# Routing weights of a PEER layer: written to DRAM one column at a time by indirect DMAs, in place of one-hot matmuls

## The chip, the cores and the metric

One core of one Trainium2 chip runs the whole layer in one launch. The metric is the device time in microseconds (us) of that launch; lower is better. All data is float32. Wide matrix products are made of three passes of the reduced type fp32r (high part times high part, high times low, low times high), so every operand is split into a high part, rounded by ScalarE, and a low part, the difference.

## The reference

One layer (DEPTH = 1) over 512 latent tokens of 2048 channels and 256 context tokens: token mixing (latent attention and a Fourier branch), then channel mixing by PEER, a retrieval over 128 x 128 = 16384 single-neuron experts. The change is in the second part:

```python
def _peer(h, wq, keys, u, v):                       # T = 512 tokens, 8 heads, 16 experts per head
    q = (hf @ wq).reshape(T, PEER_HEADS, 2, PEER_HALF)
    s = jnp.einsum('thpd,hpkd->thpk', q, keys)      # 2 x 128 scores per head
    s1, i1 = lax.top_k(s[:, :, 0], 16); s2, i2 = lax.top_k(s[:, :, 1], 16)
    cand_s = s1[..., :, None] + s2[..., None, :]    # 256 pairs of a head
    cand_i = i1[..., :, None] * 128 + i2[..., None, :]
    top_s, pos = lax.top_k(cand_s, 16)
    idx = take_along_axis(cand_i, pos); w = softmax(top_s)
    a = einsum('td,thkd->thk', h, u[idx])           # u, v: 16384 x 2048
    coef = w * gelu(a)
    return einsum('thk,thkd->td', coef, v[idx])
```

Each token so chooses 128 experts (slots). Two heads of one token can choose the same expert; its weights then add up.

## The kernel before, in words

The tokens are handled in two ways. The first 128 tokens (TS) **gather**: for each of the 128 slots GpSimd issues an indirect DMA that fetches 128 rows of u (1 MB, one row per token), VectorE forms the dot product with h (`dots`, L1673), and later the same is done with rows of v, which VectorE adds into an accumulator (`axpy`, L1686). The other 384 tokens (TD) are computed **densely** against all experts:

- Up stage: 128 blocks i of 128 experts. SyncE loads the block of u (`pu`, 1 MB, two buffers). TensorE transposes it in four quarters into PSUM (`pre_turn`, L2175), two quarters per half h. ScalarE copies a half to SBUF (`pre_copy`, L1049), then rounds it to the high part (`pre_hi`, L1056), GpSimd subtracts to get the low part (`u_low`, L698), and TensorE multiplies (`pre_up`, L114 to L116). ScalarE applies GELU (`pre_gelu`, L1061) and SyncE stores the result to `gelu_scratch`. TensorE transposes block i+1 quarter by quarter between the products of block i.
- Top-k, on VectorE during the first 26 blocks (`top_experts`, one call per 128 tokens, a chain of 21 linked steps with an exponential from ScalarE in it).
- Routing, during the next 24 blocks: `chosen` is transposed, VectorE builds one-hot matrices for four tokens at a time (96 groups; `one_hots`, L1651 to L1657), TensorE multiplies them (L2235, L2236) into a 128 x 128 map of weights per token, ScalarE copies the map out (`keep_route`, L1096), and SyncE stores it to `route_scratch` in 24 stores with runs of 256 B. The product sums duplicates by itself. Gathers of u begin after these stores have landed, because the gather ring lies over the tiles of the map.
- Down stage: 64 pairs of blocks times two halves of the channels, so 128 steps n. Each step loads 1 MB of v and 384 KB each of `gelu_scratch` and `route_scratch`; VectorE multiplies the last two (`down_coef`, L1692), ScalarE rounds v and the coefficients, VectorE takes their low parts (`down_v_lo`, `down_coef_lo`, both L1407), TensorE runs 36 matmuls of 512 columns. The `axpy` steps of the gathered tokens are put between, one per step at first and six per five steps in the second half.

The order on every engine is written out by hand: each engine runs its list in order and waits on semaphore counts. So a wait on VectorE for a gathered row also holds everything that VectorE has after it. GpSimd's list is `u_low` for both halves of a block, with one gather after five of six halves once routing is over (`gather_u`, L707), then the gathers of v (L712), which wait for a free ring buffer (four of them). SyncE's list is the loads and stores; v and coefficients for the first two down steps are fetched some 70 blocks before the end of the up stage.

## Time and profile before

| | us |
|---|---|
| median of 3 runs (lowest, highest) | 4923.87 (4911.05, 4928.48) |
| profiled execution, own time | 4906.7 |
| its span, first to last instruction | 4905.0 |
| mean granted TensorE clock, share of full | 0.963 |
| PE busy, share of the span | 4509.8 (92%) |
| DVE, ACT, POOL busy | 2843.1, 1638.3, 1395.8 |
| DMA packets, all | 652126 (967.09 MB) |

PE is TensorE (PEld its weight loads), DVE is VectorE, ACT ScalarE, POOL GpSimd, SP SyncE. The median of the runs is 17 us (0.35%) above the profiled execution. A busy PE row is made of overlapping instructions, so 92% doesn't say that TensorE does 92% of what it could: the spacing of its work tells more. In the rows below, a bracket or a last column names what ended the idle time of the engine before an instruction.

### The profile page before, as it was taken

The numbers are of one execution on the slowest core, as the hardware profiler recorded it, in microseconds if no ns is written. First come the engines' busy times: TensorE is split into PE (matmuls) and PEld (weight loads), VectorE is DVE, ScalarE is ACT, GpSimd is POOL, SyncE is SP. The second block draws the span as 40 slices with busy tenths as digits, with TensorE's granted clock in tenths as the row PEclk, the third lists the DMA queues.
The fourth block names the chain that finished last, engine by engine and source line by source line (L and its number), as shares of the span: only waits on it lengthen the run. The fifth ranks groups of instructions, "written<-read, shape, count | busy, mean of one in ns | idle before, by whom it ended". The sixth has DMA issues, their size and how long they took to land.

```text
span 4905.0 us, 61497 instructions
## 1 busy us (share of the span) xinstructions
PE 4509.8 (92%) x23115; PEld 3849.9 (78%) x23115; DVE 2843.1 (58%) x3097; ACT 1638.3 (33%) x1746; POOL 1395.8 (28%) x643
## 2 busy tenths in 40 slices
PE   7899998999989999699999999999996899999997
PEld 2587777777767877588999988999995778777776
DVE  1234665544436643657799954444444677777776
ACT  0322322333331121324446643444442233322222
POOL 0002332000002300223544556777771011011110
PEclk9899999999989999799999999999998999999998
DMA  8325664000015652453326677777776999989994
GB/s 287 96 78 172 182 184 141 18 28 30 32 39 163 189 170 61 140 167 106 122 102 162 160 235 287 290 286 287 292 283 233 349 342 345 335 315 331 338 341 166
DMA packets 652126, 967.09 MB, mean 197 GB/s; under 512 B 122203, under 2 KB 520595, under 8 KB 599571
## 3 DMA queue, kind: packets, MB, share of 16 engines
q1 hardware_dynamic: 610979, 680.35, 42.0%
q0 software_dynamic: 40928, 285.23, 16.1%
q8 instruction: 45, 0.74, 0.1%
q10 hardware_dynamic: 144, 0.52, 0.0%
q14 instruction: 30, 0.25, 0.0%
HBM read 896.82 MB, written 69.21 MB: 197 GB/s over the span
## 4 chain that ended last, share of the span: by engine, by line
PE 55%; DMA 13%; DVE 11%; issue 10%; ACT 6%; POOL 4%; SPq 1%; ACTq 0%; DVEq 0%; POOLq 0%
PE pp L114 16%; PE pp L116 15%; PE pp L115 15%; DMA gel<-gelu_scratch 10%; POOL pTul L698 3%; DVE vDl L1407 3%; PE pp L2175 3%; ACT vDh L1126 2%; DMA wm<-in_w_mod_dram 1%; PE pp L1806 1%; DVE mred L1287 1%; DVE gel L1692 1%; PE pp L1964 1%; DVE acc L1686 1%; PE pp L2236 1%
## 5 line engine op out<-in xcount | busy, mean ns | idle before, releaser
L698 POOL TENSOR_TENSOR pTul<-pT,pTuh 128x1024 fp32r<-128x1024 f32 x256 | 731.5, 2857 | 522.9 <-ACT pTuh L1056 507.2
L114 PE MATMUL pp<-h2h,pTuh 128*128 128x384 f32 x2048 | 732.9, 358 | 18.9 <-POOL pTul L698 17.4
L114 PE MATMUL pp<-vDh,coh 128*128 128x512 f32 x1536 | 614.6, 400 | 108.1 <-DVE col L1407 107.8
L116 PE MATMUL pp<-h2h,pTul 128*128 128x384 f32 x2048 | 691.7, 338 | 0.0
L115 PE MATMUL pp<-h2l,pTuh 128*128 128x384 f32 x2048 | 690.1, 337 | 0.0
L1673 DVE SCALAR_TENSOR_TENSOR ring<-ring,h2tok 128x2048 f32<-128x2048 f32 x128 | 357.6, 2796 | 480.7 <-DMA ring<-in_peer_u_dram,sidx 480.0
L115 PE MATMUL pp<-vDl,coh 128*128 128x512 f32 x1536 | 609.1, 397 | 0.0
L116 PE MATMUL pp<-vDh,col 128*128 128x512 f32 x1536 | 608.5, 396 | 0.0
L674 POOL TENSOR_TENSOR mbuf<-mbuf,silu 128x2048 f32<-128x2048 f32 x64 | 260.5, 4070 | 995.8 <-DMA mbuf<-in_w_mod_dram 995.1
L114 PEld LDWEIGHTS pp<-vDh,coh 128*128 128x128 f32 x1536 | 295.7, 193 | 187.0 <-DVE vDl L1407 73.5
L712 POOL DMA_INDIRECT ring<-in_peer_v_dram,sidx x128 | 151.7, 1186 | 938.2 <-DVE acc L1686 917.2
L114 PEld LDWEIGHTS pp<-h2h,pTuh 128*128 128x128 f32 x2048 | 388.0, 189 | 27.4 <-POOL pTul L698 27.1
L1202 DVE TENSOR_TENSOR wl<-wraw,wh 128x2048 fp32r<-128x2048 f32 (+1 forms) x97 | 263.0, 2711 | 246.8 <-ACT wh L776 246.7
L1049 ACT ACTIVATE pT<-pp 128x1024 f32<-128x1024 f32 x256 | 265.3, 1036 | 396.3 <-PE pp L2175 394.9
L115 PEld LDWEIGHTS pp<-h2l,pTuh 128*128 128x128 f32 x2048 | 388.8, 190 | 0.0
L116 PEld LDWEIGHTS pp<-h2h,pTul 128*128 128x128 f32 x2048 | 386.7, 189 | 0.0
L1407 DVE TENSOR_TENSOR vDl<-vraw,vDh 128x2048 fp32r<-128x2048 f32 x128 | 293.3, 2291 | 142.5 <-ACT vDh L1126 142.5
L1132 ACT ACTIVATE coh<-gel 128x768 fp32r<-128x768 f32 x128 | 108.5, 847 | 766.1 <-DVE gel L1692 638.4
L116 PEld LDWEIGHTS pp<-vDh,col 128*128 128x128 f32 x1536 | 295.0, 192 | 63.1
L115 PEld LDWEIGHTS pp<-vDl,coh 128*128 128x128 f32 x1536 | 296.0, 193 | 61.1
L2175 PE MATMUL pp<-ident,pu 128*128 128x128 f32 x2048 | 311.5, 275 | 18.7 <-DMA pu<-in_peer_u_dram 17.9
L114 PE MATMUL pp<-hxh,wh 128*128 128x512 f32 x784 | 315.4, 402 | 13.7 <-DVE wl L1202 9.8
(343 smaller groups left out, 8959.7 us busy)
## 6 DMA issues: line engine op xcount, KB each, us to landing
pu<-in_peer_u_dram SPq DMA_DIRECT2D x128, 1024.0 KB, 6.8
vraw<-in_peer_v_dram SPq DMA_DIRECT2D x128, 1024.0 KB, 8.1
mbuf<-in_w_mod_dram SPq DMA_DIRECT2D x64, 1024.0 KB, 5.7
wraw<-in_w_in_dram SPq DMA_DIRECT2D x48, 1024.0 KB, 8.5
wt<-route_scratch SPq DMA_DIRECT2D x128, 384.0 KB, 7.2
gel<-gelu_scratch SPq DMA_DIRECT2D x128, 384.0 KB, 9.1
wm<-in_w_mod_dram SPq DMA_DIRECT2D x16, 2048.0 KB, 8.5
gelu_scratch<-act_g SPq DMA_DIRECT2D x128, 192.0 KB, 1.9
```

The costliest lines, as they stand in the source:

```text
L114: pe.matmul(out, lh, rh, start=first, stop=False)
L115: pe.matmul(out, lh, rl, start=False, stop=False)
L116: return pe.matmul(out, ll, rh, start=False, stop=last)
L674: pool.tensor_tensor(mbuf[s][:, :, :], mbuf[s][:, :, :], silu[:, :, 0:1].to_broadcast([P, DC, P]), ALU.mult).then_inc(mu_prod, 1)
L698: pool.tensor_tensor(pTul[:, c, :], pT[:, c, :], pTuh[:, c, :].bitcast(fp32), ALU.subtract).then_inc(u_lo, 1)
L712: pool.indirect_dma_start(ring[k % 4][:, :], None, v_rows, bass.IndirectOffsetOnAxis(ap=sidx[:, k:k + 1], axis=0)).then_inc(ring_in[k % 4] ...
L1049: act.activation(pT[:, 8 * h:8 * h + 8, :], pp[h][:, :].rearrange("p (c j) -> p c j", c=8), ACT.Copy).then_inc(pre_raw, 1)
L1132: act.activation(coh[s][:, :, :], gel[s][:, :, :], ACT.Copy).then_inc(co_hi, 1)
L1202: dve.tensor_tensor(wl[s][:, 0:n, :], wraw[s][:, 0:n, :], wh[s][:, 0:n, :].bitcast(fp32), ALU.subtract).then_inc(w_lo, 1)
L1407: return dve.tensor_tensor(dst, src, hi.bitcast(fp32), ALU.subtract)
L1673: dve.scalar_tensor_tensor(out=chunks(ring[k % 4]), in0=chunks(ring[k % 4]), scalar=1.0, in1=h2tok[:, :, 0:TS], op0=ALU.mult, op1=ALU.mult ...
L2175: mm = pe.transpose(pb[q][:, P * (c % 4):P * (c % 4) + P], pu[s][:, P * c:P * c + P], ident[:, :])
```

## The change

The one-hot stage goes. After each `top_experts` call for the 384 dense tokens, VectorE runs 128 short instructions: for slot k it compares the token's 128 expert numbers with that of slot k, multiplies by the weights and sums (`accum_out`), which gives the slot the total weight of its expert. GpSimd then writes, with one indirect DMA per slot, 128 single 4 B elements into `route_scratch`, which SyncE has filled with zeros during the attention stage (8 DMAs of 3.1 MB in runs of 2 KB). There are 384 such scatters: 3 after each of blocks 18 to 35 (54), and 3 after each gather from block 36 on, until all are out (330, so 110 gathers). After every 16 scatters GpSimd waits until all earlier ones of its 128 tokens have landed.

Top-k and the summing now take the first 36 blocks (TOPS). From block 36 on ScalarE rounds the high part of u directly from PSUM and VectorE subtracts directly from PSUM (`late_hi`, `u_rest`), so GpSimd's `u_low` and ScalarE's copy end there; a PSUM half is released by VectorE. From block 36 on VectorE does one dot product after each half, in order; after block 102 it does one `axpy` after each half (50 in all), and the other 78 are spread over the down steps, never two in one. The gather ring has three buffers, not four. v and coefficients are prefetched at block 114. In the down steps `axpy` stands before `down_coef`, and ScalarE rounds v before the coefficients.

```diff
+TOPS = 36
+SCATTER_AT = 18
+EXP_AT = (5, 11, 20, 30)
+LINKS = 21
+COEF_AT = 102
+PREFETCH_AT = 114
...
+            def zero_route(p):
+                sp.dma_start(route_flat[:, bass.ds(p * ZROW, ZROW)].rearrange("j (a n) -> j a n", n=512),
+                             zeros[:, :].unsqueeze(1).to_broadcast([P, ZROW // 512, 512])).then_inc(z_stored, 16)
...
+            def gather(k):
+                if k >= 3:
+                    pool.wait_ge(ring_used, k - 2)
+                pool.indirect_dma_start(ring[k % 3][:, :], None, u_rows if k < SLOTS else v_rows,
+                                        bass.IndirectOffsetOnAxis(ap=sidx[:, k % SLOTS:k % SLOTS + 1], axis=0)
+                                        ).then_inc(ring_in[k % 3], 16)
+
+            def scatter(n):
+                b, k = n // SLOTS, n % SLOTS
+                if k == 0:
+                    pool.wait_ge(tk_chosen, b + 3)
+                elif k % TOPK == 0:
+                    pool.wait_ge(r_stored[b], 16 * k)
+                pool.indirect_dma_start(route_cells, bass.IndirectOffsetOnAxis(ap=ridx[b][:, k:k + 1], axis=0),
+                                        rw[b][:, k:k + 1], None).then_inc(r_stored[b], 16)
...
+            for i in range(SCATTER_AT, TOPS):
+                first_lows(i)
+                for _ in range(3):
+                    scatter(n)
+                    n += 1
             pool.wait_ge(tk_chosen, 2)
+            pool.wait_ge(tk_chain, SCORE_READ)
+            for k in range(2 * SLOTS):
+                gather(k)
+                for _ in range(3):
+                    if n < DB * SLOTS:
+                        scatter(n)
+                        n += 1
...
+            def late_hi(i, s, h):
+                act.wait_ge(u_turned, 2 * i + h + 1)
+                if not isinstance(i, int) or i >= TOPS + 2:
+                    act.wait_ge((u_half, a_done)[h], i - 1)
+                elif i == TOPS:
+                    act.wait_ge((u_half, a_done)[h], i)
+                elif h == 0:
+                    act.wait_ge(tk_chosen, 5)
+                act.activation(pTuh[s][:, 8 * h:8 * h + 8, :], pp[h][:, :].rearrange("p (c j) -> p c j", c=8),
+                               ACT.Copy).then_inc(u_hi, 1)
...
+                for k in range(SLOTS):
+                    if k >= 8:
+                        dve.wait_ge(tk_chain, tk.at - 7)
+                    tk.inc(dve.scalar_tensor_tensor(out=same[:, k % 8, :], in0=expert[:, :], scalar=expert[:, k:k + 1],
+                                                    in1=chosen[:, 2, :], op0=ALU.is_equal, op1=ALU.mult,
+                                                    accum_out=rw[b - 1][:, k:k + 1]))
...
+            def u_rest(i, h):
+                s = i % 2
+                c = slice(8 * h, 8 * h + 8)
+                dve.wait_ge(u_hi, 2 * i + h + 1)
+                lo(pTul[s][:, c, :], pp[h][:, :].rearrange("p (c j) -> p c j", c=8), pTuh[s][:, c, :]).then_inc(u_sub, 1)
...
+            for i in range(TOPS, NK):
+                if i == COEF_AT + 1:
+                    dve.wait_ge(scoef_set, 1)
+                    ch.link(dve.tensor_tensor(scoef[:, :], scoef[:, :], sw[:, :], ALU.mult))
+                for h in range(2):
+                    u_rest(i, h)
+                    if k < SLOTS:
+                        dot(k)
+                        k += 1
+                    elif i > COEF_AT:
+                        axpy(k - SLOTS)
+                        k += 1
...
             def ax_before(n):
+                return min(SLOTS, in_up + max(n - 2, 0) * (SLOTS - in_up + 1) // (NK - 10))
...
             for n in range(2, NK):
-                down_coef(n)
                 for k in range(ax_before(n), ax_before(n + 1)):
                     axpy(k)
+                down_coef(n)
                 down_v_lo(n)
```

## Rows read from the trace of the kernel before

**Rows 1.** The page: the chain that ended last, share of the span by engine

```profile
PE 55%; DMA 13%; DVE 11%; issue 10%; ACT 6%; POOL 4%; SPq 1%; ACTq 0%; DVEq 0%; POOLq 0%
```

**Rows 2.** Stretches (us): length, busy of PE, PEld, DVE, ACT, POOL, clock, DMA share, GB/s

```profile
2243.00:2516.00 273.00, 270.23 (x1701) 265.44 (x1700) 218.77 (x815) 131.83 (x147) 134.65 (x52) 1.00 0.32 116
2516.00:2879.00 363.00, 351.59 (x2434) 347.90 (x2435) 329.97 (x386) 211.18 (x227) 178.25 (x51) 0.99 0.62 154
2879.00:3688.00 809.00, 782.61 (x4849) 764.24 (x4847) 353.99 (x252) 345.29 (x379) 614.81 (x281) 0.99 0.77 286
3790.00:4300.00 510.00, 486.94 (x2120) 398.56 (x2119) 371.19 (x238) 155.84 (x118) 53.47 (x57) 0.98 0.94 341
4300.00:4870.00 570.00, 523.36 (x2213) 425.54 (x2212) 422.31 (x273) 164.45 (x124) 88.87 (x63) 0.96 0.85 311
```

**Rows 3.** Timeline of ACT, GELU of blocks 0, 25, 51, 127; start, duration

```profile
2254.22 0.49 ACT L1061 ACTIVATE act_g<-pp 128x384 f32<-128x384 f32 x1
...
2515.51 0.49 ACT L1061 ACTIVATE act_g<-pp 128x384 f32<-128x384 f32 x1 [1.06 <-PE pp L116]
...
2879.09 0.49 ACT L1061 ACTIVATE act_g<-pp 128x384 f32<-128x384 f32 x1 [1.07 <-PE pp L116]
...
3687.81 0.49 ACT L1061 ACTIVATE act_g<-pp 128x384 f32<-128x384 f32 x1 [5.20 <-PE pp L116]
```

**Rows 4.** The same, two GELUs five blocks apart in the late up stage

```profile
3007.52 0.49 ACT L1061 ACTIVATE act_g<-pp 128x384 f32<-128x384 f32 x1 [1.06 <-PE pp L116]
...
3058.32 0.49 ACT L1061 ACTIVATE act_g<-pp 128x384 f32<-128x384 f32 x1 [1.15 <-PE pp L116]
```

**Rows 5.** Timeline of POOL at the up stage's end: indirect DMAs in a row

```profile
3684.68 2.92 POOL L707 DMA_INDIRECT ring<-in_peer_u_dram,sidx  x1 [0.30 <-issue]
3687.90 0.93 POOL L712 DMA_INDIRECT ring<-in_peer_v_dram,sidx  x1 [0.30 <-issue]
3689.14 2.65 POOL L712 DMA_INDIRECT ring<-in_peer_v_dram,sidx  x1 [0.30 <-issue]
```

**Rows 6.** Timeline of DVE in the same stretch: the dot products

```profile
3684.50 2.29 DVE L1673 SCALAR_TENSOR_TENSOR ring<-ring,h2tok 128x2048 f32<-128x2048 f32 x1 [3.54 <-DMA ring<-in_peer_u_dram,sidx]
...
3688.69 2.29 DVE L1673 SCALAR_TENSOR_TENSOR ring<-ring,h2tok 128x2048 f32<-128x2048 f32 x1 [1.90 <-DMA ring<-in_peer_u_dram,sidx]
```

**Rows 7.** Groups of 2861:3680: count, busy us, mean ns, idle before and its releaser

```profile
L1673 DVE SCALAR_TENSOR_TENSOR ring<-ring,h2tok 128x2048 f32<-128x2048 f32 x125 | 350.7, 2809 | 473.9 <-DMA ring<-in_peer_u_dram,sidx 473.2
...
L707 POOL DMA_INDIRECT ring<-in_peer_u_dram,sidx x126 | 195.0, 1548 | 19.1 <-issue 10.0
```

**Rows 8.** DMA issues of the whole run: KB each, median us to landing

```profile
gelu_scratch<-act_g SPq DMA_DIRECT2D x128, 192.0 KB, 1.9
...
ring<-in_peer_u_dram,sidx POOLq DMA_INDIRECT x128, 7.3
```

**Rows 9.** Timeline of POOL in the top-k stretch: a low part of u

```profile
2270.39 2.39 POOL L698 TENSOR_TENSOR pTul<-pT,pTuh 128x1024 fp32r<-128x1024 f32 x1 [2.35 <-ACT pTuh L1056]
```

**Rows 10.** Timeline of DVE at the end of the first top-k call

```profile
2305.93 0.29 DVE L1633 SCALAR_TENSOR_TENSOR sidx<-tk_chosen 128x128 uint32<-128x128 f32 x1
```

**Rows 11.** Timeline of DVE, low part of v in two pairs of down steps

```profile
3889.71 2.29 DVE L1407 TENSOR_TENSOR vDl<-vraw,vDh 128x2048 fp32r<-128x2048 f32 x1 [0.53 <-ACT vDh L1126]
...
4287.62 2.29 DVE L1407 TENSOR_TENSOR vDl<-vraw,vDh 128x2048 fp32r<-128x2048 f32 x1 [2.79 <-ACT vDh L1126]
...
4341.04 2.28 DVE L1407 TENSOR_TENSOR vDl<-vraw,vDh 128x2048 fp32r<-128x2048 f32 x1
...
4793.69 2.29 DVE L1407 TENSOR_TENSOR vDl<-vraw,vDh 128x2048 fp32r<-128x2048 f32 x1 [2.28 <-ACT vDh L1126]
```

**Rows 12.** Timeline of PE: the down stage's first matmul, and two of a later step

```profile
3698.69 0.77 PE L114 MATMUL pp<-vDh,coh 128*128 128x512 f32 x1 [10.92 <-DVE col L1407]
...
4054.28 0.39 PE L114 MATMUL pp<-vDh,coh 128*128 128x512 f32 x1
4054.51 0.39 PE L115 MATMUL pp<-vDl,coh 128*128 128x512 f32 x1
```

More of the change, by code:

```diff
@@ L634, in _ @@
                     coef_loads(2 * i + s, s, 1)
-            for b in range(TB):
-                sp.wait_ge(fin_set, b + 1)
-                sp.dma_start(out[0, P * b:P * b + P, :], acc[:, b, :]).then_inc(fin_stored, 16)
+            sp.wait_ge(fin_set, 1)
+            sp.dma_start(out[0, 0:TS, :], accs[:, :]).then_inc(fin_stored, 16)
+            for b in range(DB):
+                sp.wait_ge(fin_set, b + 2)
+                sp.dma_start(out[0, TS + P * b:TS + P * b + P, :], acc[:, b, :]).then_inc(fin_stored, 16)
             sp.wait_ge(fin_stored, 16 * TB)
@@ L717, in _ @@
                 u_low(i, 1)
-            pool.wait_ge(tk_chosen, 2)
-            for ss in r_stored:
-                pool.wait_ge(ss, 64 * (TD // RT // 2) + 16)
-            k = 0
-            for i in range(LATE + 2, NK):
-                for h in range(2):
-                    u_low(i, h)
-                    if k < SLOTS and (2 * i + h) % 6 != 5:
-                        gather_u(k)
-                        k += 1
-            while k < SLOTS:
-                gather_u(k)
-                k += 1
@@ L1078, in top_block, with late_block @@
                 pre_hi(i + 1, 1)
-            for i in range(TK_FIRST):
-                top_block(i, i % 2, 1 if i == 5 else None)
+            def late_block(i, s):
+                late_hi(i + 1, 1 - s, 0)
+                pre_gelu(i, s)
+                late_hi(i + 1, 1 - s, 1)
+            for i in range(TOPS - 1):
+                top_block(i, i % 2, EXP_AT.index(i) + 1 if i in EXP_AT else None)
                 if 2 <= i < 6:
@@ L1667, in chunks, with dot @@
             def chunks(t):
                 return t[:, :].rearrange("p (c d) -> p c d", c=DC)
-            dve.wait_ge(h2_hi, DC + 4)
-            for k in range(SLOTS):
-                dve.wait_ge(ring_in[k % 4], 16 * (k // 4) + 16)
-                dve.scalar_tensor_tensor(out=chunks(ring[k % 4]), in0=chunks(ring[k % 4]), scalar=1.0,
+            def dot(k):
+                dve.wait_ge(ring_in[k % 3], 16 * (k // 3) + 16)
+                dve.scalar_tensor_tensor(out=chunks(ring[k % 3]), in0=chunks(ring[k % 3]), scalar=1.0,
@@ L2165, in _, with pre_turn @@
             mod_sum(63, 1, 6, 30)
-            def pre_turn(i, s, q):
+            def pre_turn(i, s, q, late=False):
                 if q == 0:
@@ L2214, in _ @@
             pe.wait_ge(mu_set, 4)
-            for i in range(TK_FIRST):
+            for i in range(TOPS):
                 pre_block(i, i % 2)
```

325 lines of the change are left out of this document (115 added, 210 removed).

## The prediction

> **What bounds the kernel now.** I read the chain of waits by engine first, then the stretches, then the spacing of TensorE's work. The chain lies 55% on TensorE [rows 1], and TensorE is busy for nearly all of the three up-stage stretches at a clock of 0.99 or 1.00 [rows 2]. Only the spacing says how much of that is needed. Five clean blocks of the late up stage take 3058.32 - 3007.52 = 50.8 us, so 10.16 us a block, 5.08 a half [rows 4]. The three stretches between the GELUs of blocks 0, 25, 51 and 127 take 261.3, 363.6 and 808.7 us for 25, 26 and 76 blocks: 10.45, 13.98 and 10.64 us a block [rows 3]. Over 127 x 10.16 = 1290 us the up stage loses 143 us: 7 in the top-k part, 99 in and behind routing, 37 later. In the down stage a matmul starts every 0.23 us, so a step of 36 needs about 8.2 us [rows 12]. The steps take 397.9 / 47 = 8.47 us in the first half and 452.7 / 49 = 9.24 in the second [rows 11], and the first one starts 10.9 us after the up stage ends [rows 12]. GpSimd is 76% busy in the late up stage (614.8 of 809) [rows 2]; there VectorE spends 473 us waiting for gathered rows, with the products themselves at 351 us [rows 7]. So gathering, not arithmetic, is what VectorE waits for already.
>
> **The parts that remove work.** Without one-hot matmuls, map copies, map stores and the late start of the gathers, the 99 us behind routing can go. With at most one axpy in a step, 78 rather than 128 of them, and axpy placed where VectorE waits for coefficients, I let the down steps come to 8.25 us: 47 x 0.22 + 49 x 0.99 = 59 us, rounded down to 57 because a few waits for transfers will stay. The start of the down stage no longer waits for the last dot products, since these end near block 88 to 97: 10.9 us become about 2, a gain of 9. The down stage gives 66 us; bounds are 20 (the second half stays at 9.2 because it is limited by transfers, DMA share 0.85) and 75 (every step at 8.17).
>
> **The zeros** are 25 MB in 8 stores during attention, where the page shows the DMA engines mostly idle; I take nothing. If a weight load were held by the 3.1 MB ahead of it at the 341 GB/s of [rows 2], that is 9 us each, 74 us in all at the very worst; the load goes ahead of the zeros in the queue and has a whole attention pair to land, so this stays out.
>
> **Blocks 0 to 35.** At the top-k pace, 35 intervals x 10.45 = 366 us. Added are 54 scatters on GpSimd. An indirect DMA in a row with others takes 0.93 us and 0.30 of issue, 1.24 in all [rows 5]; three are 3.7 us. They stand in front of the next low part, ahead of which GpSimd idles 2.35 us [rows 9], so up to 1.4 us a block is late and TensorE waits: about 1 us x 18 = 18, and 3 waits for landing of some 2 us, 24 us together (bounds 0 and 50). Sum: 390 us. VectorE runs beside it: four top-k calls, in the old stretch 219 us busy [rows 2], some 57 each with the part before it, and 384 summing instructions. The nearest row is a 128 x 128 operation of two inputs, 0.29 us [rows 10]; with the accumulator read, 0.37, so 142 us. 228 + 142 = 370, plus the 14 us or so that a call waits for the exponential: 384, just inside 390. The bounds are 0.21 and 0.6 us an instruction (GpSimd and VectorE delaying each other), so no stall or up to 75 us of it before block 36, where ScalarE waits for the last sum.
>
> **Blocks 36 to 88, the step that decides.** GpSimd must issue one gather and three scatters for each dot product, and VectorE's list takes one dot product per half block, in order with the subtraction that feeds TensorE. So TensorE's half can't be shorter than T, the time of GpSimd for four indirect DMAs. The trace shows no scatter; it has the same number of descriptors as a gather (one per partition), so I take the gather's 1.24 us; the bounds are 0.93 (no issue gap) and 1.9 us (the landing of a small store [rows 8], were GpSimd to wait for it). Four make 4.96 us: alone they would just fit in 5.08.
> They are not alone. The indirect DMA issued at 3684.68 began under a dot product (3684.50 to 3686.8) and took 2.92 us: it got through only 0.8 us after that had ended. The one at 3689.14 did the same (2.65), while the one at 3687.90, already under way when the product began, took 0.93 [rows 5, 6]. Over the stage the mean is 1.55 us [rows 7]. With GpSimd always issuing, each product catches one issue: in the mean the product's 2.29 less half an issue interval, 0.62; I take 1.6 us. T = 4.96 + 1.6 = 6.56.
> Then there are the waits for landing, one per 16 scatters, 20.6 in this stretch. A scatter is queued behind a gather that takes 7.3 us to land, and a lone small store takes 1.9 [rows 8]; I take 3.5, less 0.8 because a dot product can pass meanwhile: 2.7 x 20.6 / 110 = 0.5. T = 7.06 us, for 110 gathers, 53 blocks: 106 x 7.06 = 748 us.
> The Trainium skill (SBUF — State Buffer, Who interferes with whom) says that a `tensor_tensor` probe did not stall a GpSimd-issued DMA, since descriptor generation needs the write interface, as it infers. By that, T would be 5.08. The same section says that a VectorE instruction with two SBUF inputs contends with a GpSimd instruction that reads SBUF, and the indirect DMA reads its indices there: the 2.92 us row stands with this second rule.
>
> **Blocks 89 to 127** carry only gathers: 39 x 10.64 = 415 us, the old late pace, prefetch hiccup included. VectorE then does 2.4 us of product and some 1.1 us of subtraction per half, ScalarE less than before, and neither is near 5.08. That the low part (2.4 us) leaves GpSimd I count at nothing, since 10.64 contains only 0.5 us of waits of any kind. The ring of three is enough: 7.3 us to landing and 2.4 of product are 9.7, against 15.2 for three halves; without that room a half would be 9.7 / 3 = 3.2 us at least, so it never binds. Two added waits are covered likewise: VectorE's for the gathered tokens' GELU at block 103, which ScalarE computes once the products are over, has blocks 98 to 102 as cover (51 us; behind it stand the subtractions, so TensorE would stop), and SyncE's for all scatters at block 114 comes 25 blocks after the last of them.
>
> **Sum.** 390 + 748 + 415 = 1553 us against 1433.6: +119. Down stage -66. Net +53 on the profiled 4906.7: 4960. The runs' median is 17 us above that execution, so the forecast is 4977 us. In general, net = 106 T - 695 us; it is zero at T = 6.55.
>
> **Rivals.**
> *GpSimd keeps up* (T of 5.08 to 5.7). For it: four issues are 4.96 us, and two thirds of the gathers now go unblocked (a mean of 1.55 is 0.95 with 1.9 more for one in three [rows 5, 7]). Against it: the blocked rows, and that 0.12 us of room holds no landing wait. All falls to -156, with no delay before block 36 -180: 4744 to 4850 by the median.
> *GpSimd binds mildly* (T 5.7 to 6.4), if a scatter is nearer to 1.0 us or the landing waits cost nothing: 4850 to 4925.
> *The small packets or VectorE's sums are dear* (slower still). Each half brings 24 packets of 4 B per DMA engine. Routing's stores, 24 of 1 MB in 98304 packets of 256 B, took share 0.62 at 154 GB/s, where the later stage's ratio would give the block loads 0.23: 23 ns a packet [rows 2], so 0.6 us a half. If one costs 240 ns (1.9 us for eight), 5.8 us come on top of 4.5 of other traffic (1.67 MB at 286 GB/s per 0.77 of share): T = 10.3 and +397. From 50 ns the landing waits grow, T passes 7.6 near 130 ns. Or the sums cost 0.6 us each and stall 75 us. 5045 to 5250 and beyond.
> The Trainium skill (DMA: Bandwidth & Descriptors, Specifications) says that below 512 B the engine does a read-modify-write. It gives no price for 4 B; by its rule the dear end is nearer, and no trace here shows it.
> *The change doesn't do what it says*: GpSimd would still have to wait on something of routing; none is left in its list.
>
> **Chances.** Forecast (T 6.4 to 7.5; 4925 to 5045) 0.49; mild 0.14; keeps up 0.21; dear 0.16. The range leaves out half of the best case and half of the dearest: 4790 to 5110; the likeliest case's own is 4925 to 5045. About 0.3%, 15 us, can be told from no change. Faster takes keeps up and nearly all of mild, with a little for a larger down-stage gain: 0.35. Same: 0.1. Slower: 0.55.
>
> **What would show it.** Right: GELUs of blocks 40 to 85 some 14 us apart, GpSimd nearly always busy or waiting for the landing there, DMA_INDIRECT rows of 2.8 us under dot products, VectorE waiting for `ring`, then about 10.2 us a block from 90 on; down steps at 8.2 to 8.3. Wrong: 10.2 us a block from 36 on (GpSimd keeps up), a gap before block 36 with ScalarE waiting for VectorE (sums), a DMA share near 1 in that stretch (small packets), or a second half of the down stage still at 9.2.

## The result, and the profile after

The changed kernel takes 4946.74 us (median of 13 runs, 4938.44 to 4960.93), the kernel before in the same measurement 4923.87 (13 runs, 4911.05 to 4935.42): a ratio of 1.0052, 95% interval 1.0041 to 1.0063. It is 23 us slower. I had forecast 4977 us, 53 us slower. The sign was right, and so was the mechanism by which the up stage gets longer; the down stage gains more than I had it. The profiled execution of the changed kernel has an own time of 4955.31 us and a span of 4953.5, at a clock of 0.947.

First the chain of the page, to be held against [rows 1]. TensorE's share is larger, and GpSimd has 12% of the chain where it had 4%:

```profile
PE 61%; POOL 12%; DVE 10%; issue 8%; DMA 4%; ACT 3%; SPq 0%; DVEq 0%; ACTq 0%; POOLq 0%
PE pp L116 19%; PE pp L118 18%; PE pp L117 18%; POOL route_scratch L700 8%; DVE tk_same L1623 4%; POOL ring L690 3%; DMA wm<-in_w_mod_dram 1%; PE pp L1793 1%; PE pp L2162 1%; DVE mred L1271 1%; DMA route_scratch<-rw,ridx 1%; PE pp L1951 1%;
```

The GELUs on ScalarE of blocks 0, 35, 36, 88 and 127 give the length of each part, as [rows 3] did before:

```profile
2266.18 0.49 ACT L1065 ACTIVATE act_g<-pp 128x384 f32<-128x384 f32 x1
...
2664.98 0.49 ACT L1065 ACTIVATE act_g<-pp 128x384 f32<-128x384 f32 x1 [9.40 <-remote]
2709.18 0.49 ACT L1065 ACTIVATE act_g<-pp 128x384 f32<-128x384 f32 x1 [8.76 <-PE pp L118]
...
3413.00 0.49 ACT L1065 ACTIVATE act_g<-pp 128x384 f32<-128x384 f32 x1 [6.05 <-PE pp L118]
...
3830.09 0.49 ACT L1065 ACTIVATE act_g<-pp 128x384 f32<-128x384 f32 x1 [1.65 <-PE pp L118]
```

So 398.8 us to block 35, 44.2 for block 36, 703.8 for 52 blocks (13.54 each), 417.1 for the last 39 (10.69 each). The stretches beside them (length; busy of PE, PEld, DVE, ACT, POOL; clock; DMA share; GB/s):

```profile
2250.00:2665.00 415.00, 380.16 (x2339) 371.47 (x2337) 386.69 (x1542) 177.65 (x197) 247.93 (x132) 0.96 0.33 112
2665.00:2709.00 44.00, 13.05 (x65) 12.58 (x66) 26.25 (x74) 2.41 (x3) 25.87 (x21) 0.61 0.41 145
2709.00:3413.00 704.00, 589.75 (x3329) 565.43 (x3327) 354.01 (x310) 126.58 (x157) 540.23 (x417) 0.92 0.71 247
3413.00:3830.00 417.00, 398.23 (x2480) 392.28 (x2480) 250.18 (x170) 96.87 (x119) 65.57 (x70) 0.98 0.81 297
```

In the third one TensorE does the same work as anywhere, in a third more time, and nothing in the columns is full: GpSimd has 540 of 704 us. The clock of 0.92 goes with TensorE's waits; it is 1.00 over these blocks when the waits are gone (e1, below). The groups of that stretch show why that is full all the same (count; busy us, mean ns; idle before, releasers):

```profile
L700 POOL DMA_INDIRECT route_scratch<-rw,ridx x312 | 391.4, 1254 | 132.1 <-issue 91.8 <-DMA route_scratch<-rw,ridx 40.3
...
L1645 DVE SCALAR_TENSOR_TENSOR ring<-ring,h2tok 128x2048 f32<-128x2048 f32 x104 | 238.4, 2293 | 350.2 <-DMA ring<-in_peer_u_dram,sidx 344.8 <-issue 5.4
...
L690 POOL DMA_INDIRECT ring<-in_peer_u_dram,sidx x105 | 149.3, 1422 | 32.0 <-issue 32.0
L2162 PE MATMUL pp<-ident,pu 128*128 128x128 f32 x832 | 139.9, 295 | 114.1 <-DVE pTul L1391 114.0
```

GpSimd's two rows sum to 391.4 + 132.1 + 149.3 + 32.0 = 704.8 us, the whole stretch. "Idle, issue" before an indirect DMA is not free time. The chain runs backwards through the rows: TensorE waits for VectorE's subtraction, which stands behind a dot product, which waits 345 us for gathered rows, which GpSimd issues too slowly. Its timeline in the middle of the stretch:

```profile
3000.87 0.98 POOL L690 DMA_INDIRECT ring<-in_peer_u_dram,sidx  x1 [0.30 <-issue]
3002.15 2.20 POOL L700 DMA_INDIRECT route_scratch<-rw,ridx  x1 [0.30 <-issue]
3004.65 0.96 POOL L700 DMA_INDIRECT route_scratch<-rw,ridx  x1 [0.30 <-issue]
3005.92 0.96 POOL L700 DMA_INDIRECT route_scratch<-rw,ridx  x1 [0.30 <-issue]
3007.18 2.21 POOL L690 DMA_INDIRECT ring<-in_peer_u_dram,sidx  x1 [0.30 <-issue]
3009.70 0.98 POOL L700 DMA_INDIRECT route_scratch<-rw,ridx  x1 [0.30 <-issue]
3015.83 2.71 POOL L700 DMA_INDIRECT route_scratch<-rw,ridx  x1 [5.15 <-DMA route_scratch<-rw,ridx]
```

and VectorE's beside it:

```profile
3001.21 2.29 DVE L1645 SCALAR_TENSOR_TENSOR ring<-ring,h2tok 128x2048 f32<-128x2048 f32 x1 [4.16 <-DMA ring<-in_peer_u_dram,sidx]
...
3006.26 2.29 DVE L1645 SCALAR_TENSOR_TENSOR ring<-ring,h2tok 128x2048 f32<-128x2048 f32 x1 [1.61 <-DMA ring<-in_peer_u_dram,sidx]
```

A scatter costs 0.96 + 0.30 us, as a gather does. The one that begins at 3002.15, under the product of 3001.21 to 3003.50, ends at 3004.35, 0.85 us after the product; so does the gather at 3007.18 (end 3009.39, product's end 3008.55). Of the 416 indirect DMAs of the stretch, the 99 that begin under a product take 2.35 us in the mean, the other 317 take 0.97. The landing wait at 3015.83 is 5.15 us. With 0.96 + 0.30 for each of four, a half block of 6.77 us is 5.04 of issuing, 1.35 of delay under products ((391.4 + 149.3 - 417 x 0.96) / 104) and 0.39 of landing waits (40.3 / 104): 6.78.

The 44 us of block 36 are on VectorE:

```profile
2640.46 0.35 DVE L1623 SCALAR_TENSOR_TENSOR tk_same<-tk_expert,tk_chosen 128x128 f32<-128x128 f32 x1
...
2640.73 2.54 DVE L1623 SCALAR_TENSOR_TENSOR tk_same<-tk_expert,tk_chosen 128x128 f32<-128x128 f32 x1
...
2679.80 0.35 DVE L1623 SCALAR_TENSOR_TENSOR tk_same<-tk_expert,tk_chosen 128x128 f32<-128x128 f32 x1
...
2690.07 2.29 DVE L1645 SCALAR_TENSOR_TENSOR ring<-ring,h2tok 128x2048 f32<-128x2048 f32 x1 [2.95 <-DMA ring<-in_peer_u_dram,sidx]
...
2692.28 1.22 DVE L1391 TENSOR_TENSOR pTul<-pp,pTuh 128x1024 fp32r<-128x1024 f32 x1
```

The last summing instruction is at 2679.80, four products follow, the fourth of them waits for its rows, and only then comes the first subtraction of the new scheme, at 2692.28, for which TensorE has waited 34 us. A lone sum goes by at 0.27 us, but the one at 2640.73 took 2.54. GpSimd had begun a low part just then:

```profile
2640.74 2.39 POOL L680 TENSOR_TENSOR pTul<-pT,pTuh 128x1024 fp32r<-128x1024 f32 x1 [1.46 <-ACT pTuh L1049]
```

The down stage is the gain. Low parts of v on VectorE, steps 6, 63, 66 and 127:

```profile
3910.71 2.29 DVE L1391 TENSOR_TENSOR vDl<-vraw,vDh 128x2048 fp32r<-128x2048 f32 x1 [10.26 <-ACT vDh L1114]
...
4387.82 2.29 DVE L1391 TENSOR_TENSOR vDl<-vraw,vDh 128x2048 fp32r<-128x2048 f32 x1 [1.87 <-ACT vDh L1114]
...
4412.87 2.29 DVE L1391 TENSOR_TENSOR vDl<-vraw,vDh 128x2048 fp32r<-128x2048 f32 x1 [1.09 <-ACT vDh L1114]
...
4910.61 2.29 DVE L1391 TENSOR_TENSOR vDl<-vraw,vDh 128x2048 fp32r<-128x2048 f32 x1 [4.12 <-ACT vDh L1114]
```

That is 477.1 / 57 = 8.37 us a step in the first half and 497.7 / 61 = 8.16 in the second, where the kernel before took, over the same steps of its trace, 8.67 and 9.10. From the last GELU to the end of the span are 1123.4 us, before 1217.2.

### The profile page after: what moved, and what is told of

Its sections match the earlier page's. It is cut to its first block, busy times and chain, and to the rows that moved or that the text cites. A ratio compares the mean times of both kernels' runs of the same rounds, so it can differ in the third digit from the quotient of the medians.

```text
span 4953.5 us, 59127 instructions
## 1 busy us (share of the span) xinstructions
PE 4470.3 (90%) x22338; PEld 3812.0 (77%) x22338; DVE 2831.8 (57%) x3664; ACT 1349.0 (27%) x1465; POOL 1295.3 (26%) x844
## 4 chain that ended last, share of the span: by engine, by line
PE 61%; POOL 12%; DVE 10%; issue 8%; DMA 4%; ACT 3%; SPq 0%; DVEq 0%; ACTq 0%; POOLq 0%
PE pp L116 19%; PE pp L118 18%; PE pp L117 18%; POOL route_scratch L700 8%; DVE tk_same L1623 4%; POOL ring L690 3%; DMA wm<-in_w_mod_dram 1%; PE pp L1793 1%; PE pp L2162 1%; DVE mred L1271 1%; DMA route_scratch<-rw,ridx 1%; PE pp L1951 1%; POOL pTul L680 1%; ACT wh L767 1%; DMA pu<-in_peer_u_dram 1%
## 5 line engine op out<-in xcount | busy, mean ns | idle before, releaser
L116 PE MATMUL pp<-h2h,pTuh 128*128 128x384 f32 x2048 | 753.4, 368 | 18.2 <-POOL pTul L680 18.0
L118 PE MATMUL pp<-h2h,pTul 128*128 128x384 f32 x2048 | 709.6, 346 | 0.0
L117 PE MATMUL pp<-h2l,pTuh 128*128 128x384 f32 x2048 | 708.2, 346 | 0.0
L116 PE MATMUL pp<-vDh,coh 128*128 128x512 f32 x1536 | 603.5, 393 | 40.6 <-DVE col L1391 40.3
L700 POOL DMA_INDIRECT route_scratch<-rw,ridx x384 | 472.8, 1231 | 157.4 <-issue 109.8
L1645 DVE SCALAR_TENSOR_TENSOR ring<-ring,h2tok 128x2048 f32<-128x2048 f32 x128 | 293.1, 2291 | 364.3 <-DMA ring<-in_peer_u_dram,sidx 358.8
L2162 PE MATMUL pp<-ident,pu 128*128 128x128 f32 x2048 | 327.9, 285 | 186.7 <-DVE pTul L1391 154.0
L2162 PEld LDWEIGHTS pp<-ident,pu 128*128 128x128 f32 x2048 | 263.3, 147 | 222.9 <-DVE pTul L1391 172.7
L1114 ACT ACTIVATE vDh<-vraw 128x2048 fp32r<-128x2048 f32 x128 | 245.3, 1917 | 677.4 <-PE pp L118 653.7
L116 PEld LDWEIGHTS pp<-h2h,pTuh 128*128 128x128 f32 x2048 | 403.2, 197 | 21.2 <-POOL pTul L680 13.2
L117 PEld LDWEIGHTS pp<-h2l,pTuh 128*128 128x128 f32 x2048 | 403.5, 197 | 0.0
```

Source lines behind the costliest of these rows:

```text
L116: pe.matmul(out, lh, rh, start=first, stop=False)
L117: pe.matmul(out, lh, rl, start=False, stop=False)
L118: return pe.matmul(out, ll, rh, start=False, stop=last)
L700: pool.indirect_dma_start(route_cells, bass.IndirectOffsetOnAxis(ap=ridx[b][:, k:k + 1], axis=0), rw[b][:, k:k + 1], None).then_inc(r_stor ...
L1114: act.activation(vDh[s][:, :, :], vraw[s][:, :, :], ACT.Copy).then_inc(w_hi, 1)
L1645: dve.scalar_tensor_tensor(out=chunks(ring[k % 3]), in0=chunks(ring[k % 3]), scalar=1.0, in1=h2tok[:, :, 0:TS], op0=ALU.mult, op1=ALU.mult ...
```

## The experiments

The runs in one table. "Half" is half of the mean block between the GELUs of blocks 36 and 88; "up" is from the first GELU to the last; "down" from there to the end of the span. Each kernel ran beside the kernel before; those with the same time in the column "before" ran on one chip together. Where the hand-over is at block 42 (e8, e9, e11, e12), "half" mixes five blocks of the early scheme and the hand-over with the rest; over blocks 42 to 88 alone these four have 6.92, 5.72, 5.56 and 5.60, the kernel after 6.79.

| kernel | before, us | this, us | ratio (95%) | half | up | down |
|---|---|---|---|---|---|---|
| before, profiled | | | | 5.87 | 1433.6 | 1217.2 |
| after, profiled | 4923.87 | 4946.74 | 1.0052 (1.0041-1.0063) | 6.77 | 1563.9 | 1123.4 |
| r1_before_again | 4944.39 | 4940.77 | 0.9997 (0.9985-1.0010) | 5.89 | 1438.9 | 1236.9 |
| e1_no_late_scatters | 4944.39 | 4757.84 | 0.9627 (0.9611-0.9643) | 5.07 | 1365.8 | 1122.7 |
| e2_short_dots | 4944.39 | 4833.49 | 0.9777 (0.9761-0.9793) | 5.80 | 1444.5 | 1125.9 |
| e5_rotated | 4944.39 | 4910.52 | 0.9935 (0.9919-0.9952) | 6.49 | 1515.1 | 1123.6 |
| r2_after_again | 4936.29 | 4947.34 | 1.0018 (1.0007-1.0029) | 6.83 | 1557.0 | 1122.2 |
| e6_before_down_order | 4936.29 | 4864.64 | 0.9848 (0.9830-0.9867) | 5.91 | 1441.7 | 1166.1 |
| e10_old_down_order | 4936.29 | 4980.54 | 1.0080 (1.0059-1.0101) | 6.82 | 1559.3 | 1156.7 |
| e9_all | 4936.29 | 4822.31 | 0.9765 (0.9742-0.9789) | 5.95 | 1437.9 | 1127.9 |
| e3_two_per_gather | 4941.83 | 4870.00 | 0.9856 (0.9840-0.9873) | 6.02 | 1481.6 | 1122.7 |
| e8_tops42_only | 4941.83 | 4939.02 | 0.9996 (0.9983-1.0010) | 7.04 | 1544.2 | 1125.6 |
| e11_no_gap | 4941.83 | 4817.09 | 0.9748 (0.9732-0.9764) | 5.55 | 1423.1 | 1123.9 |
| e12_no_burst | 4940.16 | 4801.96 | 0.9719 (0.9703-0.9735) | 5.59 | 1406.8 | 1125.9 |

**Is the second stretch GpSimd's, and what is in its half block?**

e1 takes the scatters from block 36 on away; it leaves out the 330 late routing weights.

```diff
             for k in range(2 * SLOTS):
                 gather(k)
-                for _ in range(3):
-                    if n < DB * SLOTS:
-                        scatter(n)
-                        n += 1
```

> The changed kernel with the 330 scatters from block 36 on left out (so most routing weights stay zero); the gathers stay. My theory, that four indirect DMAs of GpSimd per half block set the pace (13.5 us a block from 36 to 88): blocks there fall to 10.2 or 10.3 us, 52 x 3.25 = 169 us less, about 4780 us. Rival 1, that the pace comes from VectorE's new place in front of TensorE (a PSUM half is released only after its subtraction, with the dot products in the same list): blocks stay near 13.5 us, about 4945 us. Rival 2, small packets that crowd the DMA engines: the same gain as by my theory; this run doesn't tell the two apart.

e2 leaves the scatters and makes the products short; it leaves out 15 of each dot product's 16 chunks.

```diff
-  dve.scalar_tensor_tensor(out=chunks(ring[k % 3]), in0=chunks(ring[k % 3]), scalar=1.0,
-                           in1=h2tok[:, :, 0:TS], ...
+  dve.scalar_tensor_tensor(out=chunks(ring[k % 3])[:, 0:1, :], in0=chunks(ring[k % 3])[:, 0:1, :],
+                           scalar=1.0, in1=h2tok[:, 0:1, 0:TS], ...
```

> The changed kernel with each dot product taken over the first 128 of 2048 channels only (the rest of it is left out), so VectorE holds its two-operand instruction for some 0.3 us, not 2.29; gathers and scatters are all issued. My theory (the product blocks the start of an indirect DMA, 1.35 us a half, and beside it come 5.06 us of issue and 0.4 of landing waits): a half falls from 6.77 to about 5.5 us, so blocks 36 to 88 from 13.5 to 11.0 us, about 130 us less, 4815 us. Rival (the scatters' small packets delay the gathered rows, or landing waits dominate): the transfers are unchanged, so no change beyond 20 us, about 4935 us.

e5 keeps scatters, products and waits but takes the 16 scatters between two waits from the three blocks of tokens in turn, so that a wait is for scatters of which the last was issued 32 earlier.

```diff
+  order = list(range(3 * (TOPS - SCATTER_AT)))
+  ... # then groups of TOPK from the three token blocks in turn
-  b, k = n // SLOTS, n % SLOTS
+  b, k = order[n] // SLOTS, order[n] % SLOTS
```

> The changed kernel with the order of the scatters from block 36 on changed: groups of 16 of the three token blocks in turn, so that the wait for the landing of earlier scatters of the same tokens is nearly always over when it is reached. Same scatters, same gathers. By the waits of the changed kernel's trace (40 us in 11 waits from block 36 to 88) I expect 30 to 40 us less, 4910 us. Rival (small packets set the pace; the wait only moves to the gathered rows): no change, 4945 us.

Without late scatters the same 52 blocks take 10.14 us each, and TensorE is busy for all of it:

```profile
2705.00:3230.00 525.00, 525.00 (x3315) 518.06 (x3315) 352.00 (x311) 126.43 (x156) 96.34 (x103) 1.00 0.91 329
```

GpSimd's rows of e2 from 2707 to 3310 us, then of e5 from 2704 to 3378 (stretches as long as blocks 36 to 88 are there, but begun 13 us late):

```profile
L700 POOL DMA_INDIRECT route_scratch<-rw,ridx x304 | 294.0, 967 | 162.6 <-issue 88.1 <-DMA route_scratch<-rw,ridx 74.5
L690 POOL DMA_INDIRECT ring<-in_peer_u_dram,sidx x107 | 104.5, 977 | 39.1 <-issue 31.1 <-DVE ring L1645 8.1
```

```profile
L708 POOL DMA_INDIRECT route_scratch<-rw,ridx x306 | 371.3, 1213 | 93.2 <-issue 93.2
L690 POOL DMA_INDIRECT ring<-in_peer_u_dram,sidx x106 | 170.9, 1613 | 37.5 <-issue 31.7 <-DVE ring L1653 5.8
```

In e2 the mean issue is 0.967 and 0.977 us: the delay is gone with the long products, so it was theirs. The landing waits grow from 40.3 to 74.5 us, which gives back 0.33 of the 1.35 us a half; 5.80 is left, where I had written 5.5. In e5 the landing waits are gone and the issues stay long (1.2 and 1.6 us), so a half falls by only 0.28 of the 0.39. The small packets don't set the pace: e2 moves the same packets in 603 us as the kernel after in 704, and its half is made up by GpSimd's own rows. What share they have in the landing waits is not shown. Take all the late scatters away (e1) and TensorE is the bound.

**One scatter less.** e3 has two behind a gather and a third behind every fourth.

```diff
-  for _ in range(3):
+  for _ in range(DB * SLOTS - n if k == SLOTS + 2 else 3 if k % 4 == 0 else 2):
```

> The kernel after with one edit: two scatters behind a gather and a third behind every fourth, rather than three behind each; the last 38 go together behind the third gather of the value rows. Theory (GpSimd's list sets the half block, one scatter costs about 1.26 us of it, landing waits are shared): a half of 6.77 us falls by 0.75 x 1.26 + 0.1 = 1.05 to about 5.7, blocks 36 to 88 at 11.4 us each (-111 us), the scatters and dot products last some ten blocks longer at the same pace (+10), in all 85 to 110 us faster than the kernel after: a ratio of 0.980 to 0.986. Rival (the small packets delay the block loads whatever the issue rate): the pace falls in proportion to the packets only, to 12.7 us a block, and half of that comes back later: under 40 us of gain.

A half falls by 0.75 us, to 6.02, where I expected 5.7: the three quarters of a scatter bring 0.95, but the delay per product grows from 1.35 to 1.49 us (by the same sum from e3's trace), and the landing waits stay (43.8 us). The gain is 82 us of the up stage, a ratio of 0.9856, at the least gain that I had written (0.980 to 0.986). Its rival (under 40 us) is out.

**The hand-over.** e8 moves it to block 42.

```diff
-TOPS = 36
+TOPS = 42
-EXP_AT = (5, 11, 20, 30)
+EXP_AT = (5, 11, 22, 33)
-COEF_AT = 102
+COEF_AT = 106
```

> The kernel after with the hand-over from the top-k scheme to the late scheme at block 42, not 36, and the exponentials of top-k blocks 2 and 3 behind blocks 22 and 33, not 20 and 30. Theory: the sums end near block 37, so ScalarE's wait at the hand-over goes (34 us at block 36), as do its waits of 11 and 15 us at blocks 20 and 30; what is left at the hand-over is the first gather, 20 to 25 us at block 42; 18 scatters more are done before it, so three blocks fewer run at 13.5 us (-9). In all 30 to 55 us faster than the kernel after, a ratio of 0.992 to 0.996. Rival: these waits are covered by VectorE's or GpSimd's later work being the bound anyway (the blocks behind end at the same time): under 10 us of gain.

My expectation failed. Block 36 is reached after 388.2 us, where it was 443.0, but 34 of these us were the hand-over, and it has only moved: block 42 takes 43.0 us, as block 36 took 44.2, where I had expected 20 to 25. VectorE waits there for the rows of four products in a row, 20.5 us for the first. The waits for the exponential shrank and did not go (blocks 23 and 34 take 17.7 and 18.0 us; blocks 20 and 30 took 21.2 and 25.2). GpSimd's first gather comes at 2701.1 us, in the kernel after at 2657.5, and its last scatter at 3419.0, there at 3409.8: the list starts 44 us later and, 18 scatters shorter, takes 34 us less, with three more blocks done at its end. The pace in it is no better (6.92 us a half over blocks 42 to 88, against 6.79). The up stage is only 13 to 20 us shorter than in the two profiles of the kernel after, and the ratio is 0.9996 where the forecast was at most 0.996. Its rival fits best: the later blocks wait for GpSimd's list, and that began later.

e9 is e3, e5 and e8 in one. e11 and e12 follow from its trace.

> The changed kernel mended where the theory says it loses: TOPS 42 rather than 36 (top-k and sums no longer end after the early blocks), the exponentials at blocks 22 and 33 rather than 20 and 30, COEF_AT 106, from there 2 scatters after a gather and 3 after every fourth (the rest after the last gather of u), and the scatter groups of 16 in turn over the three token blocks. Theory: the gap of 34 us at block 36 and 26 us of waits before it go; a half block takes 3.25 issues of 1.27 us and 1.35 of blocking, 5.5 us, so 11 us a block for 62 blocks rather than 13.5 for 52 and 10.2 for 10: about 100 us less; with the landing waits, 150 to 180 us below the changed kernel, ratio to before 0.97. Rival, that dot products and scatters collide as often as there are products, so that fewer scatters per gather don't help: 60 to 80 us less, ratio 0.99.

It came to 4822.31 us, a ratio of 0.9765, where the kernel after has 1.0018 on the same chip: 125 us less, short of the 150 to 180 expected and well over the rival's 60 to 80. Block 42 took 35.3 us, on a wait for the first gathered row:

```profile
DVE ring L1653 <- DMA ring<-in_peer_u_dram,sidx: 40.8, 5, 30.5
ACT pTuh L1067 <- PE pp L2170: 26.7, 1, 26.7
PEld pp L2170 <- DVE pTul L1399: 23.2, 1, 23.2
```

so e11 issues three gathers ahead of block 41's low parts and drops the four products ahead of the first subtraction:

```diff
             for i in range(SCATTER_AT, TOPS):
+                if i == TOPS - 1:
+                    pool.wait_ge(tk_chosen, 2)
+                    pool.wait_ge(tk_chain, SCORE_READ)
+                    for k in range(3):
+                        gather(k)
                 first_lows(i)
 ...
-            while k < 4:
-                dot(k)
-                k += 1
```

> e9_all with two edits: the first three gathers stand ahead of block 41's low parts in GpSimd's list, and the four dot products ahead of the first subtraction of the late scheme are gone (they follow with two a block as the others). Theory: in e9_all block 42 took 35.3 us because VectorE waited 30 us there for the first gathered row and TensorE waited for VectorE; with the gathers on their way before, the block takes 10 to 14 us and the kernel gains 20 to 25 us on e9_all, a ratio of about 0.971 to 0.973. Rival: the top-k's sums are what comes late (VectorE reaches that place too late in any case), then the gap stays at 20 us or more and the ratio at 0.976.

The gap at block 42 went (10.6 us there), but the up stage became only 15 us shorter than in e9 (1423.1 against 1437.9), the ratio 0.9748 against 0.9765, short of the 0.971 to 0.973 expected: block 109 now took 33.0 us.

```profile
POOL ring L690 <- DVE accs L1668: 39.3, 10, 6.8
...
DVE accs L1668 <- DMA ring<-in_peer_v_dram,sidx: 24.0, 2, 23.8
PEld pp L2170 <- DVE pTul L1402: 20.2, 1, 20.2
```

The scatters left over, issued in one go behind the third gather of v (`k == SLOTS + 2` in e3's edit), keep the next gathers of v back: some 28 of them at 1.26 us are 35 us. e12 takes the burst away:

```diff
-  for _ in range(DB * SLOTS - n if k == SLOTS + 2 else 3 if k % 4 == 0 else 2):
+  for _ in range(3 if k % 4 == 0 else 2):
```

> e11_no_gap with one edit: the scatters that are left behind the third gather of the value rows aren't issued in one go there but go on at two behind a gather (a third behind every fourth) until none is left, near block 112. Theory: in e11_no_gap block 109 took 33 us, since VectorE's axpy waited 23.8 us for value rows whose gathers stood behind some 25 scatters in a row (1.26 us each) in GpSimd's list, and TensorE waited for the subtraction behind that axpy. Without the burst the block takes some 11 us and the kernel gains 18 to 23 us on e11_no_gap: a ratio of 0.970 to 0.972. Rival: the prefetch stop at block 115 (28 us in e11_no_gap), which waits for the last scatter's landing, grows by as much as the burst gives back: 0.975.

It came to 4801.96 us, a ratio of 0.9719, in the range written (0.970 to 0.972), though the gain on e11 is 14 us by the ratios and not 18 to 23. The stop at block 115 stayed as it was (27.9 us in both). e12 is the fastest version: 138 us under the kernel before on the same chip. GpSimd's rows from 2706 to 3300 us, blocks 41 to 93, still fill the time (594.9 us of 594), so it is still the bound there:

```profile
L708 POOL DMA_INDIRECT route_scratch<-rw,ridx x235 | 340.9, 1451 | 71.6 <-issue 71.6
L690 POOL DMA_INDIRECT ring<-in_peer_u_dram,sidx x104 | 146.6, 1410 | 35.8 <-issue 31.1 <-DVE ring L1656 4.7
```

**The down stage.** e6 is the kernel before with two edits: in a down step `axpy` before `down_coef` and v before the coefficients on ScalarE, and the 128 axpys spread evenly.

```diff
             def down_pair(n, s):
+                down_v(n, s)
                 down_coef(n, s)
-                down_v(n, s)
...
             def ax_before(n):
-                if n < 2:
-                    return 0
-                if n <= PAIRS:
-                    return n - 2
-                return min(SLOTS, PAIRS - 2 + (n - PAIRS - 2) * 6 // 5) if n > PAIRS + 2 else PAIRS - 2
+                return min(SLOTS, max(n - 2, 0) * SLOTS // 120)
...
             for n in range(2, NK):
-                down_coef(n)
                 for k in range(ax_before(n), ax_before(n + 1)):
                     axpy(k)
+                down_coef(n)
```

> The kernel before with one part of the change alone: in each down step axpy stands before down_coef, ScalarE rounds v before the coefficients, and the 128 axpys are spread evenly over the steps (7 steps have two, where the kernel before has some ten), nothing else. If order and even spacing bring the down stage's gain (94 us against the first profiled execution), this kernel is 80 to 110 us faster than before, 0.980. Rival: the gain comes from having 78 axpys and gathers in place of 128 (less traffic, the DMA share was 0.85 to 0.94): then it gains 30 us or less.

e10 is the kernel after with the old order and its own spacing (the first and the last part of this diff, reversed).

> The changed kernel with the old order in its down steps (down_coef before axpy on VectorE, coefficients before v on ScalarE), still with 78 axpys, never two in a step. If the order is what brings the steps to 8.16 us, they go back to some 8.5 us and the kernel is 40 us slower than the changed one; if the fewer axpys and gathers do, the steps stay at 8.2 and the time within 10 us of it.

Low parts of v, steps 66 and 127, in e6 and then in e10:

```profile
4321.89 2.29 DVE L1407 TENSOR_TENSOR vDl<-vraw,vDh 128x2048 fp32r<-128x2048 f32 x1
...
4826.45 2.29 DVE L1407 TENSOR_TENSOR vDl<-vraw,vDh 128x2048 fp32r<-128x2048 f32 x1 [4.12 <-ACT vDh L1126]
```

```profile
4427.84 2.29 DVE L1391 TENSOR_TENSOR vDl<-vraw,vDh 128x2048 fp32r<-128x2048 f32 x1 [0.53 <-ACT vDh L1114]
...
4937.11 2.29 DVE L1391 TENSOR_TENSOR vDl<-vraw,vDh 128x2048 fp32r<-128x2048 f32 x1 [2.79 <-ACT vDh L1114]
```

e6 takes 8.27 us a step there, before 9.10 to 9.28; its down stage is 71 us shorter than r1's (1166.1 against 1236.9; 51 shorter than the 1217.2 of the first profile) and its time 72, just short of the 80 to 110 expected; the rival (30 or less) is out. e10 takes 8.35, and its down stage is 34.5 us longer than r2's (1156.7 against 1122.2), its time 33, where I had expected 40. So in the kernel after, order is worth 33 us. What order and spacing take away is a chain of waits. The longest in the second half of the kernel before (4341 to 4793 us), then in e6 (4322 to 4826), as total, times, longest:

```profile
ACT coh L1132 <- DVE gel L1692: 240.9, 35, 12.1
DVE gel L1692 <- DMA gel<-gelu_scratch: 90.0, 24, 7.8
...
PEld pp L114 <- DVE vDl L1407: 41.6, 11, 5.3
```

```profile
DVE gel L1692 <- DMA gel<-gelu_scratch: 80.0, 39, 6.4
...
ACT coh L1132 <- DVE gel L1692: 61.9, 42, 3.4
...
PEld pp L114 <- DVE vDl L1407: 5.1, 2, 2.6
```

ScalarE no longer stands still for VectorE's coefficients before it rounds v, and TensorE hardly waits for v's low part. VectorE waits for the GELU transfer as before. Transfers don't hold the second half at 9.1 us: e6 moves 170.1 MB over steps 66 to 127 at 337 GB/s, the kernel before 175.8 MB at 317. The first half is another matter: e6 takes 8.80 us a step there, before 8.67 and 8.88 in its two profiles, with the DMA engines 94% busy at 346 GB/s. The kernel after takes 8.37, with 149.2 MB over those steps in place of e6's 173.6; whether the transfers hold e6 there is not shown.

Order and even spacing together give 71 without any other part of the change; the remaining 44 of 115 (1236.9 - 1122.2) come with the rest, which is 50 fewer axpys in this stage and a start without the 10.9 us of [rows 12] (the first down matmul now waits 0.63 us). No run parts these two, nor the spacing from the order in the kernel before.

**What the measurement itself does.** r1 is the kernel before and r2 the kernel after, each with a profile of its own.

> The kernel before, once more, for a second profiled execution of it. The two profiled executions differ by 48.5 us in span where the medians of the runs differ by 22.9: if the first profiled execution of before was a quick one, this one has a span of 4915 to 4930 us, and the stretches in which it is longer show where executions differ; if it comes at 4905 again, the profiled execution of the changed kernel was a slow one.

> The changed kernel once more, beside the kernel before on the same chip, for a second profiled execution and a second ratio. The ratio should come near 1.005 again. In the two profiled executions of before the down stage took 1217 and 1237 us after the last GELU, in the one of the changed kernel 1123: if the changed kernel's is bound by TensorE, its steps come at 8.16 us again and the stage within 3 us of 1123.

r1's span is 4938.4 us, 33 longer than the profile that I forecast from and above the 4915 to 4930 that I had expected, at the clock of 0.959 (0.963 there). 8.4 of it lie before the first GELU, 5.3 in the up stage and 19.7 in the down stage. Part of the 33 us belongs to the measurement and not to the one execution: the kernel before has a median of 4923.87 us in the first one and of 4936 to 4944 in the later ones. r2's span is 4942.8. The change in spans is +48.5 us for the first pair and +4.4 for the second; by the times it is +22.9 us, 0.52% (0.41 to 0.63), in the first measurement and 0.18% (0.07 to 0.29) in r2's, where I had expected 0.5% again. The two intervals don't meet, so the change costs 0.2 to 0.5%, and these runs say no more.

## Why the prediction was right or wrong

- **Blocks 0 to 35: 390 us, measured 398.8 and 389.3.** Right in the number by luck, not by its terms. ScalarE waited 11 and 15 us for the top-k chain at blocks 20 and 30 (11 and 10 in r2), which I had at nothing. My 24 us of late low parts hardly show: the other 33 blocks take 10.68 us in the mean (10.55 in r2), 8 and 3 us in all above the pace of 10.45.
- **The sums: no stall taken, 0 to 75 us as bounds, 34 measured.** I took 0.37 us an instruction. Alone it is 0.27; beside GpSimd's low parts and scatters the runs of 128 took 58 to 67 us, 0.46 to 0.52 each; over 384 that is 44 us more than at 0.37, and the last sum came at 2680. This was a miss of the centre, on the side that I had named, "GpSimd and VectorE delaying each other". The four products ahead of the first subtraction, which I had not counted, are 12 of the 34 us.
- **The step that decides, T = 7.06 us a half, measured 6.77 (r2 6.83).** Right in mechanism, 4% high. Term by term: issuing 4.96 against 5.04, the delay under a product 1.6 against 1.35 (e2 removes it), landing 0.5 against 0.39 (e5 removes it; 0.47 in r2). Over 104 halves, 0.29 us make 30 us too many.
- **Blocks 89 to 127: 415 us, measured 417.1 and 413.3.** Right. The ring of three and the GELU at block 103 (10.1 us) cost nothing. The prefetch does: block 115 takes 26.8 us, in the kernel before 10.3, and TensorE waits 14.0 of them for a block of u, whose load stands behind the prefetch in SyncE's list. It isn't the wait for the late scatters, since e1 has none and takes 25.9 there. My old pace of 10.64 held two such stops (blocks 53 and 58, 21.9 and 24.9 us), so the number came out.
- **The up stage: +119 us, measured +130 and (r2 less r1) +118.** The total was right by luck: block 36 took 30 us more than the 14.1 that T gave it, and the smaller T took 30 us off the other 52 blocks.
- **The down stage: -66 us, measured -94 on the profiled pair and -115 on the second pair. This is the step that failed: the gain per down step was sized too small and summed over too few steps.** "I let the down steps come to 8.25 us: 47 x 0.22 + 49 x 0.99 = 59 us, rounded down to 57." The sum covered 96 of 127 steps; the 31 between and beside the two windows of [rows 11] were taken to gain nothing. Over all of them the first profile gives (8.67 - 8.37) x 57 + (9.10 - 8.16) x 61 = 74 us, and 19 more lie in the start (10.3, where I had 9), in steps 0 to 6 (6.5) and in steps 63 to 66 (1.8). The upper bound of 75, "every step at 8.17", had the same gap. That the second half would come off 9.2 was right: it comes to the matmuls' own 8.16, and e6 shows that most of this is order and spacing. Between r1 and r2 the down stage is the whole miss: start +1, up +118, down -115 make +4, where I had +119 and -66.
- **The base.** The forecast was made on one execution and moved to the median by adding 17 us. The down stage of the kernel before can be 20 us longer (r1), and the changed kernel's is not: 1123.4, 1122.2, and 1122.7 to 1127.9 in every run with its down stage. So the quick execution understated what could be won. In numbers: forecast +53 us, first pair of own times +48.6 (up 11 too little, start of the up stage +12 that I did not count, down 28 too little gain); of these, 17 are the profile of before lying under its median and 9 that of after lying above its own, which leaves +23. The +12 is not the zeros: between r1 and r2 the up stage starts 1.1 us later.
- **The rivals.** The borders in us don't all follow from my formula: net = 106 T - 695 puts T = 6.4 at 4907 us and 7.5 at 5024, where I wrote 4925 and 5045. With the measured T of 6.77 the formula gives 4946, the measured time; that is chance, since it leaves out the stall at block 36 and has the down stage's gain too small. "GpSimd keeps up" is out: 6.77 against 5.08. "Mild" (T below 6.4) too. "Small packets dear" is out by e2; "sums dear" is half true (0.5 us a sum, 34 us).
- **The Trainium skill** (SBUF — State Buffer, Who interferes with whom): it tells of a probe in which a `tensor_tensor` did not stall a GpSimd-issued DMA. Carried over to this kernel's products, a `scalar_tensor_tensor` with two SBUF inputs, that doesn't hold (2.20 us against 0.96 for a scatter that begins under a product); the section's other rule, two SBUF inputs on VectorE against a GpSimd instruction that reads SBUF, does. The subtractions with one input in PSUM (1.22 us each) delay nothing that can be seen: in e2, where all of them are in place, the mean issue is 0.967 us. The rule of the Trainium skill (DMA: Bandwidth & Descriptors, Specifications) on what is below 512 B, a read-modify-write, had no visible price in the pace at 24 packets of 4 B per engine and half block (e2).

## What to carry to other kernels

Count what each engine has to issue per step of the bound engine, at the full pitch (here 1.26 us per indirect DMA, whatever it carries), and add what the neighbour's long instructions hold up; where the sum passes the step, spread the issues over more steps before anything else. Time gained ahead of such a list is lost again where the list itself starts later by it (e8), and leftovers put in one burst become a gap for whoever stands behind them (e11). A hand-over that is moved keeps its gap until the first issues are put ahead of it (e9 against e11). Forecast from two executions of the kernel before where there are two, and sum a gain over all steps of a stage, not over the windows that happened to be read.

## What the runs showed of the hardware that I had not expected

- An indirect DMA of 128 elements of 4 B costs GpSimd the same 0.96 us and 0.30 of gap as one of 128 rows of 8 KB (0.98).
- An indirect DMA that begins under a two-input VectorE product in SBUF ends 0.85 us after the product. Each product of 2.29 us so takes 1.35 to 1.6 us of GpSimd's time when GpSimd always has a next one (1.35 in the kernel after, 1.49 in e3, 1.58 in e12); at 16 times shorter products it is 0.04 (e2: (294.0 + 104.5 - 411 x 0.96) / 104).
- It works in the other direction as well: a 128 x 128 sum on VectorE at a pitch of 0.27 us takes 2.54 when GpSimd's low part (2.39 us) begins just then.
- The landing waits grew when GpSimd became quicker: 40.3 us in 11 waits in the kernel after and 48.9 in 16 in r2, 74.5 in 17 in e2.
- Two profiled executions of the kernel before, in two measurements, differ by 33 us in the span at nearly the same mean clock, 20 of them in the down stage, where all runs with the down stage of the kernel after keep within 6 us.
